# Softmax attention with the value block stationary and the turned weights moving, two heads at a time

## The reference

```
def causal_block_attention(q_nope, q_rope, k_nope, k_rope, v):
    for i in range(s // Q_BLOCK):                    # 2 blocks of 128 queries
        sc = (q_nope . k_nope + q_rope . k_rope) * QK_DIM ** -0.5
        sc = where(ki <= qi, sc, -inf)
        p = softmax(sc, axis=-1)
        outs.append(einsum("bhqk,bkhd->bhqd", p, v[:, :kend]))
    return concatenate(outs, axis=1)
...
    return o.reshape(b, s, MLA_HEADS * V_DIM) @ w_out
```

## Time and profile before

| | before |
|---|---|
| median of 3 executions | 1731.38 us |
| the profiled execution | 1730.71 us |
| its span | 1729.0 us |
| PE busy | 1714.8 us, 99% |
| DVE busy | 1202.6 us, 70% |
| ACT busy | 872.4 us, 50% |
| POOL busy | 98.8 us, 6% |
| DMA | 298.27 MB, mean 173 GB/s |

### The profile page before, as it was taken

The page is one execution under the profiler, slowest core; times in us unless marked ns, Lnnn a source line. Parts: engine busy times, 40 slices in busy tenths (PEclk is TensorE's granted clock), DMA queues, the critical chain, the costliest instruction groups (busy, mean ns, idle before and its releaser), DMA issues.

```text
span 1729.0 us, 24831 instructions
## 1 busy us (share of the span) xinstructions
PE 1714.8 (99%) x9528; PEld 1486.5 (86%) x9528; DVE 1202.6 (70%) x1379; ACT 872.4 (50%) x1085; POOL 98.8 (6%) x141
## 2 busy tenths in 40 slices
PE   9999999999999999999999999999999999999998
PEld 7888899888888888889888888988887888888887
DVE  7667799675766777667767767886557765567676
ACT  5434575765443444336864434765337634454343
POOL 0000031130000000001500000000000100000000
PEclk9999999999999999999999999999999999999999
DMA  7564465324556464553336465464564464436543
GB/s 260 184 208 168 154 210 166 120 98 146 197 192 202 166 213 166 201 189 113 134 112 220 164 209 187 159 203 135 186 194 139 154 194 146 171 134 219 204 166 115
DMA packets 215425, 298.27 MB, mean 173 GB/s; under 512 B 13557, under 2 KB 171322, under 8 KB 215354
## 3 DMA queue, kind: packets, MB, share of 16 engines
q1 hardware_dynamic: 215290, 297.27, 51.7%
q10 hardware_dynamic: 64, 0.02, 0.0%
HBM read 296.21 MB, written 1.05 MB: 172 GB/s over the span
## 4 chain that ended last, share of the span: by engine, by line
PE 91%; DVE 3%; issue 3%; ACT 1%; DMA 1%; POOL 0%; SPq 0%; DVEq 0%; POOLq 0%
PE PS L474 26%; PE PS L480 14%; PE PS L349 12%; PE PS L350 12%; PE PS L426 7%; PE PS L368 4%; PE PS L466 2%; PE PS L461 1%; PE PS L462 1%; PE PS L343 1%; PE PS L345 1%; PE PS L344 1%; DVE wlo L332 1%; PE PS L774 1%; DVE conv_acc L1199 1%
## 5 line engine op out<-in xcount | busy, mean ns | idle before, releaser
L327 ACT ACTIVATE whi<-raw 128x2048 fp32r<-128x2048 f32 (+3 forms) x286 | 534.5, 1870 | 465.3 <-PE PS L480 367.5
L332 DVE TENSOR_TENSOR wlo<-raw,whi 128x2048 fp32r<-128x2048 f32 (+3 forms) x286 | 635.5, 2238 | 123.9 <-ACT whi L327 123.5
L474 PE MATMUL PS<-XT,whi 128*128 128x512 f32 x2016 | 472.1, 390 | 1.7 <-DVE XT L889 1.7
L474 PEld LDWEIGHTS PS<-XT,whi 128*128 128x128 f32 x2016 | 376.5, 188 | 79.9 <-issue 2.9
L480 PEld LDWEIGHTS PS<-XT,wlo 128*128 128x128 f32 x2016 | 252.1, 191 | 5.9
L480 PE MATMUL PS<-XT,wlo 128*128 128x256 f32 x2016 | 255.0, 283 | 0.0
L705 DVE TENSOR_REDUCE ff_s<-PS 128x512 f32<-128x1024 f32 x55 | 67.3, 1224 | 208.7 <-PE PS L480 198.9
L350 PE MATMUL PS<-whi,aT 128*128 128x512 f32 x400 | 156.3, 391 | 0.0
L349 PE MATMUL PS<-whi,aT 128*128 128x512 f32 x400 | 156.2, 390 | 0.0
L349 PE MATMUL PS<-whi,XT 128*128 128x512 f32 (+2 forms) x320 | 125.7, 394 | 0.0
L350 PE MATMUL PS<-whi,XT 128*128 128x512 f32 (+2 forms) x320 | 122.2, 383 | 0.0
(11 more groups left out here) (434 smaller groups left out, 2197.4 us busy)
## 6 DMA issues: line engine op xcount, KB each, us to landing
raw<-in_w_in SPq DMA_DIRECT2D x112, 512.0 KB, 4.5
raw<-in_ffn_w_up SPq DMA_DIRECT2D x88, 512.0 KB, 5.1
raw<-in_ffn_w_down SPq DMA_DIRECT2D x88, 512.0 KB, 4.4
raw<-in_ffn_w_gate SPq DMA_DIRECT2D x86, 512.0 KB, 4.5
raw<-in_ssm_w_in SPq DMA_DIRECT2D x48, 512.0 KB, 4.6
raw<-in_w_ffn_in SPq DMA_DIRECT2D x44, 512.0 KB, 4.3
raw<-in_w_ffn_out SPq DMA_DIRECT2D x22, 512.0 KB, 4.2
raw<-in_ssm_w_out SPq DMA_DIRECT2D x16, 512.0 KB, 4.0
```

Source lines behind the costliest of these rows:

```text
L327: act.activation(whi[s][:, 0:size], raw[s][:, 0:size], ACT.Copy).then_inc(hi_done, 1)
L332: dve.tensor_tensor(wlo[s][:, 0:size], raw[s][:, 0:size], whi[s][:, 0:size].bitcast(FP32), ALU.subtract).then_inc(lo_done, 1)
L474: return pe.matmul(o, whi[n % SLOTS][:, sl], XT[:, k, :, :].rearrange("p a n -> p (a n)"), start=(k == 0), stop=False)
```

## The change

The second product of the attention is grouped and turned round. `pair_out` takes two heads at once: the values of a head (128 keys x 64 features) are stationary, its turned weights move (256 queries, then the 128 queries that see the second half of the keys), and the result is 64 features x 256 queries, the first head in partitions 0 to 63 of the bank and the second in partitions 64 to 127. That is already the side on which the output projection wants it, so `out_done` and `turn_out` go, and ACT and DVE split the bank of the outputs itself. The sums can no longer be divided out of the result, where a query is a column; so DVE divides the exponentials by their sum (`divide`, new semaphore `pn`) before PE turns them. The core of the diff:

```
+        def outputs_of(b):
+            return psS.rearrange("p (k n) -> p k n", k=2)
...
-            def head_out(g):
-
-                pe.wait_ge(M["ptc"], g + 1)
+            def pair_out(g):
+
+                pe.wait_ge(M["ptc"], g + 2)
                 if g % 4 == 0:
                     pe.wait_ge(M["vcopied"], g // 4 + 1)
                     if g:
-                        pe.wait_ge(M["od"], g // 4)
-                o = [psS[:, t * 256 + (g % 4) * DV:t * 256 + (g % 4 + 1) * DV] for t in range(NT)]
-                pe.matmul(o[0], probT[:, g % 2, 0:P], v_nat[:, 0, g, :], start=True, stop=True)
-                pe.matmul(o[1], probT[:, g % 2, P:2 * P], v_nat[:, 0, g, :], start=True, stop=False)
-                pe.matmul(o[1], probT[:, g % 2, 2 * P:TRI], v_nat[:, 1, g, :], start=False, stop=True).then_inc(M["o"], 1)
+                        pe.wait_ge(M["ll"], g // 4)
+                o = [psS[j * DV:(j + 1) * DV, g % 4 // 2 * SEQ:(g % 4 // 2 + 1) * SEQ] for j in range(2)]
+                for j in range(2):
+                    pe.matmul(o[j], v_nat[:, 0, g + j, :], probT[:, j, 0:SEQ], start=True, stop=False)
+                for j in range(2):
+                    m = pe.matmul(o[j][:, P:SEQ], v_nat[:, 1, g + j, :], probT[:, j, SEQ:TRI], start=False, stop=True)
+                m.then_inc(M["o"], 1)
 
             def turn_prob(g):
-                pe.wait_ge(M["e"], 2 * g + 2)
+                pe.wait_ge(M["pn"], g + 1)
...
-            def turn_out(b):
...
-                if h >= 2:
-                    head_out(h - 2)
+                if h >= 3 and h % 2:
+                    pair_out(h - 3)
...
-                if h in OUT_TURN:
-                    turn_out(OUT_TURN[h])
             project_part(9)
-            turn_out(3)
...
             def left_hi(b):
-                act.wait_ge(M["lt"], b + 1)
+                act.wait_ge(M["o"], 2 * b + 2)
...
                     if g >= 2:
-                        act.wait_ge(M["o"], g - 1)
+                        act.wait_ge(M["o"], g // 2)
                     act.activation(probT[:, g % 2, :], psT[:, 0:TRI], ACT.Copy).then_inc(M["ptc"], 1)
+                if h in (5, 9, 13):
+                    left_hi(h // 4 - 1)
...
-            def out_done(g):
...
+            def divide(h):
+
+                dve.wait_ge(M["e"], 2 * h + 2)
+                own.link(dve.reciprocal(rsum[:, :, h], psum_[:, :, h]))
+                for t, sl in enumerate((slice(0, P), slice(P, TRI))):
+                    m = dve.tensor_scalar(prob[:, h % 2, sl], prob[:, h % 2, sl], rsum[:, t, h:h + 1], None, ALU.mult)
+                m.then_inc(M["pn"], 1)
...
+                if h in (6, 10, 14):
+                    left_lo(h // 4 - 1)
...
+                if h < MH:
+                    divide(h)
             left_lo(3)
```

More of the change, by code:

```diff
@@ L1457, in build @@
         M = sems("mla", "kro in gain1 trig_in trig_out mask sq var r cn ct ch cl qcopied sqq sqk vcopied qv kv qr kr rot roped qn qp krr kb kn "
-                        "turned tc s nm e pt ptc o od lt lh ll")
+                        "turned tc s nm e pn pt ptc o lh ll")
         RW = KVL + DR
@@ L1507, in build @@
         FILL_ORDER = FIRST_FILLS + [FILLS[h] for h in sorted(FILLS)]
-        OUT_TURN = {7: 0, 11: 1, 14: 2}
-        OUT_BANK = [3, 5, 5, 5]
+        def outputs_of(b):
+            return psS.rearrange("p (k n) -> p k n", k=2)
         def fill_count(kind, g, half):
@@ L1634, in project_part @@
                 b, t, k = p // 4, 1 - p // 2 % 2, p % 2
+                if p == 0:
+                    pe.wait_ge(M["qcopied"], 4)
                 if p % 4 == 0:
@@ L1756, in left_hi @@
             def left_hi(b):
-                act.wait_ge(M["lt"], b + 1)
-                act.activation(XTh[:, 2 * b:2 * b + 2, :], PS[:, OUT_BANK[b], :].rearrange("p (k n) -> p k n", k=2), ACT.Copy)\
-                   .then_inc(M["lh"], 1)
+                act.wait_ge(M["o"], 2 * b + 2)
+                act.activation(XTh[:, 2 * b:2 * b + 2, :], outputs_of(b), ACT.Copy).then_inc(M["lh"], 1)
             for h in range(MH + 2):
@@ L1763, in mla_act @@
                     turned(*FILLS[h])
-                if h == 12:
-                    left_hi(1)
                 if h < MH:
@@ L1792, in mla_act @@
                 if h == 8:
-                    left_hi(0)
                     kv_copy(3)
@@ L1800, in mla_act @@
                     hi_upto(act, at, N["mla_out"] + 3)
-                if h == 15:
-                    left_hi(2)
                 if h == 16:
@@ L1902, in left_lo @@
                 dve.wait_ge(M["lh"], b + 1)
-                dve.tensor_tensor(XTl[:, 2 * b:2 * b + 2, :], PS[:, OUT_BANK[b], :].rearrange("p (k n) -> p k n", k=2),
+                dve.tensor_tensor(XTl[:, 2 * b:2 * b + 2, :], outputs_of(b),
                                   XTh[:, 2 * b:2 * b + 2, :].bitcast(FP32), ALU.subtract).then_inc(M["ll"], 1)
-            def out_done(g):
[L1908 to L1913, removed]
+            def divide(h):
[4 more added lines that the diff above has]
+                m.then_inc(M["pn"], 1)
             for h in range(MH + 2):
@@ L1937, in mla_dve @@
                 if h == 5:
-                    out_done(0)
                     k_norm(2)
@@ L1945, in mla_dve @@
                     q_norm(3)
-                    left_lo(0)
                     k_sums(3)
-                if h == 9:
-                    out_done(1)
                 if h == 10:
@@ L1953, in mla_dve @@
                     lo_upto(dve, at, N["mla_out"] + 1)
-                if h == 12:
-                    left_lo(1)
                 if h == 13:
-                    out_done(2)
                     lo_upto(dve, at, N["mla_out"] + 2)
```

## The result

| | before | after |
|---|---|---|
| median of 7 runs each, us | 1731.27 (1730.83 to 1731.57) | 1737.34 (1734.54 to 1738.1) |
| profiled execution, us (span) | 1730.71 (1729.0) | 1734.54 (1732.8) |
| last output product (L345) of the stage starts, us | 896.80 | 900.40 |

The ratio is 1.0033, 95% interval 1.0022 to 1.0043: slower by a third of a per cent. The median lies 2.0 us above the forecast of 1735.3 us and inside the stated range of 1731.0 to 1739.0. The profiled execution is the fastest of the seven: it took 3.83 us more than that of before, where the sum had +3.9; the other six took 1736.2 to 1738.1. So there are two results to explain, the 3.8 us that the trace shows, and 1.7 to 3.6 us more in the other six, 2.8 in the median, that it does not.

The account below looks back on a forecast made before the run. PE was taken to bound the kernel. Saving 5.6 us against waits of 9.5 gave +3.9, from 1730.71 to 1734.6 profiled, plus 0.67 for the median: 1735.3 us, 0.22% slower, range 1731.0 to 1739.0.

Parts of the forecast that it names:

- the sum: Whole execution: saving 5.6 against waits 9.5, +3.9 us, profiled execution 1734.6, median 0.67 above it.
- What bounds it: Attention stage: PE is busy 63.51 of 64 us, so its waits and gains both go to the end.
- The saving: PE in the attention stage: output products and turns removed, paired products added; 4.1 to 7.2 us less, taken as 5.6.
- row halves: Differential attention's products on halves of the contraction rows, taken as model for a pair: 1.05 us, saving 4.1.
- Rows 6: Products with 36 stationary columns, next one 0.11 behind without a gap; read as no mode-change cost, giving the 7.2 saving.
- The waits: PE at the turns of the weights, waiting for DVE's division: 9.5 us taken, between 10.1 and 9.0.
- The row for a saving of 4.1: Waits at the turns if PE saves 4.1: 0.6 each at heads 3, 11 and 13, none at 7, 9.0 in all.
- they add up to 8 to 10 us: Sign to look for: PE's waits for DVE at the turn of the weights total 8 to 10 us.
- Cost of `divide`: DVE, per head from start to end: 0.7 us, or 1.2 where POOL works, mostly steps 0 to 7.
- A: Rival: column halves run one after the other, +6.3 us, 1737.7 us; chance 0.26.
- B: Rival: turns find the division done, 1724.2 to 1725.8 us, or 1728.1 if heads 8 and 14 alone wait; chance 0.09.
- C: Rival: half the waits, lateness from POOL and at heads 3, 6, 11, 13 made up; 5.6 us, 1731.4; chance 0.13.

Follow-up runs that it names:

- experiment 10: Changed kernel with the turn of the weights and everything behind it one step later, and the division one step later, right behind the maxima: 1729.75 us, ratio 0.9992.
- experiment 2: Changed kernel without the division, the turn waiting for the exponential alone: 1728.87 us, ratio 0.9984.
- experiment 3: Kernel before with the division alone, old output products and turns kept, outputs copied without scaling: 1737.82 us, ratio 1.0046.
- experiment 8: Changed kernel with both heads of a pair on the same column half, one after the other: 1741.46 us, ratio 1.0061.
- experiment 1: Changed kernel again without an edit: 1738.12 us, ratio 1.0042; its profiled execution was one of the long ones.
- experiment 5: Changed kernel with four useless two-pass products of 256 columns ahead of the turn of head 8: 1735.44 us, ratio 1.0025.
- experiment 4: Changed kernel with the division ahead of DVE's other duty in steps 8 and 14 alone: 1733.05 us, ratio 1.001.
- experiment 6: Changed kernel with the division ahead of DVE's other duty in step 8 alone: 1735.92 us, ratio 1.0023.
- experiment 9: Changed kernel with the turn of the weights and everything behind it one step later, three weight buffers, division left in its step: 1733.15 us, ratio 1.001.
- experiment 7: Changed kernel with the division ahead of DVE's other duty in step 14 alone: 1735.96 us, ratio 1.0029.

## Why the prediction was right, and where it was off

**What bounds it.** Right: PE's microseconds went to the end one for one. In all twelve profiles the execution's time less the stage's end lies between 833.9 and 834.3 us.

**The saving.** Taken 5.6, the middle of 4.1 and 7.2. From the turn to the second product of a 512-column step it is 1.58 us in experiment 10 (860.32 to 861.90), less 0.56 of a step without a product 1.02, where the row halves had given 1.05. Eight pairs are 8.2, and 1.8 + 10.7 - 8.2 = 4.3 us. So the lower of the two ends was the right one, and the term was mis-sized by 1.3. What decided is that a group on column halves pays beyond its columns nearly what one on row halves pays: 0.09 in front, and 0.80 instead of the 0.66 of its columns (0.1, and 0.86, with row halves). Rows 6 misled: 36 stationary columns among products of 128 do not show that cost. The Trainium skill, "TensorEngine Tiling (Array Packing)", section "Tiling Modes", says that a change of tiling mode drains the engine, and the trace of after agrees with its 0.09 us: following the rule alone would have given 4.1. The Trainium skill, "TensorE: Matmul & The Clock Gate", section "Part 3: Packing small matmuls", has column tiles at work side by side, three of them in its measurement; this case agrees in kind, 1.44 / 0.80 = 1.8 times for two. Net of the waits that the faster engine meets (0.9 at one turn, for ACT's copy), 3.2 are left (experiment 2).

**The waits.** Taken 9.5 for a saving of 5.6, and 9.0 for one of 4.1. With a saving of 4.3 and a stage 3.6 longer they are 7.9, by subtraction; the waits view gives 6.5 for DVE on PE itself, and 9.1 on its weight loads, which overlap. Experiments 2 and 3 give the whole price of the division, 6.8 and 6.9. The two long ones are where they were forecast and of that size: 1.83 at head 8 (carried 2.1) and 1.61 at head 14 (1.8). The row for a saving of 4.1 had 0.6 at heads 3, 11 and 13, where 0.61, 0.64 and 0.54 came. The early ones were carried too long: 0.8 at head 0, 0.6 at 1 and 1.1 at 6 against 0.56, 0.18 and 0.49, and those at 2 and 4 are not there. (The waits listed for 4.1 add up to 8.7 and not to 9.0; that would make the sum +3.8 or so.) The sign "they add up to 8 to 10 us" did not come in the waits view, with its 6.5; what makes the rest of the 7.9, beside 0.3 at one of the scores, is open. Both errors have one sign and nearly cancel, 1.3 too much saved and 1.6 too much waited: that the profiled execution met the +3.9 to a tenth is luck in part.

**Cost of `divide`.** From 860.47 to 861.22 it is 0.75 us, forecast 0.7. The 1.2 beside POOL did not come (ns min, median, max over both shapes):

```profile
L1895 DVE TENSOR_SCALAR prob<-prob,rsum x32: 285/342/567, 832.6 to 885.4; 128x128 f32<-128x128 f32 x16, 128x256 f32<-128x256 f32 x16
```

Fifteen of the 16 pairs of scalings take 0.55 or 0.56 us, also where POOL is busy with its roots (L1970), and only that of head 5, beside POOL's rotations (L1964, L1965), takes 0.90:

```profile
835.95 2.91 POOL L1970 TENSOR_TENSOR head_rs<-head_var,neghalf 128x16 f32<-128x16 f32 x1
852.39 0.46 POOL L1965 TENSOR_TENSOR q_nat<-rtmp 128x128 f32<-128x128 f32 x1
```
```profile
838.46 0.55 DVE L1895 TENSOR_SCALAR prob<-prob,rsum 128x128 f32<-128x128 f32 x2
852.11 0.90 DVE L1895 TENSOR_SCALAR prob<-prob,rsum 128x128 f32<-128x128 f32 x2
```

The row that the forecast took its 1.2 from stood beside POOL's work on 256 columns, and was carried to all of POOL's time. That 0.5 us too much in the early steps is of the size by which the waits at heads 0 to 6 were carried too long.

**The rivals.** A fell with experiment 8, and its price was near: that profile less the clock's 3.4 us is 1738.1, where A had 1737.7. B was a matter of order, as forecast, and not of DVE's room: experiment 10 is this rival made true, though it ends at 1729.75 and not at 1728.1 or less, since DVE and ACT still hold PE at single heads. C came in one of its two halves: the lateness from POOL is gone, that at heads 3, 6, 11 and 13 stayed, and the waits of 7.9 lie between C's 5.6 and the forecast's 9.5.

**The term that was missing.** The sum worked with one clock, and put the median 0.67 above the profiled execution, where it lies 2.8 above. In the profile of experiment 1 PE was at its lower level for 6.8 us, which cost 3.46 us at the stage's end; that most other executions of the changed kernel owe their length to the same is inferred from their times and from mean clocks of 0.997 to 0.999. Shown are: the lower clock in the records (experiments 1 and 8), that all three such stretches begin within 1 us of the end of the longest waits, of 1.72 to 1.85 us, that useless work in the place of that wait goes with shorter runs (5), and that without both long waits the top group is gone (4, against experiment 1 in the same series of runs). Against a long wait as the whole cause stands experiment 3: behind the longest of all, 2.42 us, the clock stayed up, and three of five runs are short. Before has long runs too: 4 of the 60 taken beside the experiments lie at 1733.1 to 1733.8, with a mean clock of 0.998, and its profile has no wait above 0.8 us in the stage. All four stand in the one series that experiments 5, 6, 8 and 9 belong to, so series differ, and experiments 4, 6 and 7, compared above, come from three of them. Not shown is at which head it falls in the runs without a trace, and why runs with the same waits differ. The versions without long waits keep a spread of about 2 us (1727.5 and 1729.5 in experiment 2, 1728.8 to 1730.8 in 10), whose cause stays open too.

## What to carry to other kernels

A producer put at the end of a step that feeds the start of the next costs what stands ahead of it, not what it takes itself: here 0.75 us of work a head cost 6.8 us of the stage behind the duty, and 1.2 us one step later, right behind what the next consumer needs (stage ends 900.40 and 894.84, against 893.64 without the division). When a consumer is moved to give slack, move the producer's place in its own queue as well (experiment 9 against 10). And where the busiest engine gets waits of nearly 2 us that it didn't have, count the clock as a possible term of its own: here the loss went from 3.8 us in the profiled execution to 6.1 in the median, and the clock is what one trace shows for the difference.

## What the hardware showed that was not expected

- Two-pass products on the two column halves start within 20 ns of each other and take 0.80 us a pair, against 1.44 on one half. 0.09 us pass between the turn and such a group, 0.1 with row halves.
- After a wait of 1.8 us the granted clock fell to half for 7 us in one execution and not at all in another of the same kernel with the same waits. The loss (3.46 us) was larger than the wait. After a wait of 2.42 us, in experiment 3, it did not fall.
- With four useless products of 256 columns, two-pass, in the place of a wait the median was 1.9 us lower, in another series of runs.
- Two scalings of 128 and 256 columns on DVE take 0.55 us while POOL works on its roots, and 0.90 beside its rotations.
